# A block with a 16384-expert layer: gathered experts replaced by dense products over both tables, split fp32r products replaced by plain fp32 ones

## The reference

```python
q = (xt @ wq).reshape(t, 8, 2, 128)
scores = einsum('thpd,hpnd->thpn', q, keys)         # 8 heads, 2 halves, 128 keys
s_top, i_top = top_k(scores, 16)
cand = s_top[:, :, 0, :, None] + s_top[:, :, 1, None, :]
c_score, c_idx = top_k(cand, 16)
expert = i1 * 128 + i2                              # of 16384
gates = softmax(c_score)
a = gelu(einsum('td,thkd->thk', x, u_tab[expert]))  # 128 rows a token
y = einsum('thk,thkd->td', gates * a, v_tab[expert])
```

## Time and profile before

| | us |
|---|---|
| median of 3 runs | 1440.13 (1437.09 to 1442.69) |
| the profiled execution | 1454.04 |
| its span, first to last instruction | 1452.3 |

### The profile page before, as it was taken

The page is one execution under the profiler, slowest core; times in us unless marked ns, Lnnn a source line. Parts: engine busy times, 40 slices in busy tenths (PEclk is TensorE's granted clock), DMA queues, the critical chain, the costliest instruction groups (busy, mean ns, idle before and its releaser), DMA issues.

```text
span 1452.3 us, 13572 instructions
## 1 busy us (share of the span) xinstructions
PE 962.3 (66%) x4844; PEld 709.2 (49%) x4844; DVE 932.9 (64%) x1773; ACT 371.8 (26%) x769; POOL 634.8 (44%) x591
## 2 busy tenths in 40 slices
PE   5998996440714505566635073077899996999996
PEld 4797885110201202252511021027667784999996
DVE  3458367868887689787796985742353214888743
ACT  4544222110101101111011010012133123777632
POOL 2015027777775677778777758870001002000000
PEclk9999999785966858679868577599985588999998
DMA  4563569999999899999999989992500011555440
GB/s 161 183 181 119 211 234 391 351 356 372 342 410 336 313 372 345 344 340 337 361 364 346 398 302 319 316 376 73 193 1 0 1 55 62 174 175 174 160 160 30
DMA packets 137044, 353.60 MB, mean 243 GB/s; under 512 B 19952, under 2 KB 43664, under 8 KB 136848
## 3 DMA queue, kind: packets, MB, share of 16 engines
q0 software_dynamic: 73728, 268.47, 50.1%
q1 hardware_dynamic: 62000, 84.02, 17.1%
q10 hardware_dynamic: 1248, 0.23, 0.1%
HBM read 351.64 MB, written 1.05 MB: 243 GB/s over the span
## 4 chain that ended last, share of the span: by engine, by line
PE 41%; POOL 23%; DVE 15%; DMA 9%; issue 9%; ACT 2%; another core or an unknown queue 0%; SPq 0%; POOLq 0%; DVEq 0%; ACTq 0%
POOL high L1845 13%; POOL arena L1845 10%; PE ps L381 7%; PE ps L385 7%; PE ps L382 7%; DVE arena L1116 3%; PE ps L581 3%; DMA high<-in_v_tab,ids 2%; PE ps L595 2%; DMA high<-in_u_tab,ids 2%; PE ps L774 2%; PE ps L552 2%; PE ps L746 2%; DMA arena<-in_v_tab,ids 2%; DMA arena<-in_u_tab,ids 2%
## 5 line engine op out<-in xcount | busy, mean ns | idle before, releaser
L581 PE MATMUL ps<-high,arena 128*128 128x512 f32 x292 | 159.2, 678 | 248.5 <-ACT arena L1572 136.9
L581 PEld LDWEIGHTS ps<-high,arena 128*128 128x128 f32 x292 | 57.7, 214 | 347.2 <-ACT arena L1572 189.3
L581 PE MATMUL ps<-arena 128*128 128x512 f32 x220 | 122.8, 690 | 154.4 <-ACT arena L1572 65.7
L1093 DVE CUSTOM_DVE_ANT_0 high<-high,arena 128x1024 f32<-128x1024 f32 x145 | 177.2, 1225 | 36.2 <-DMA high<-in_u_tab,ids 31.2
L1845 POOL DMA_INDIRECT high<-in_v_tab,ids x147 | 170.5, 1160 | 60.4 <-issue 41.9
L1845 POOL DMA_INDIRECT high<-in_u_tab,ids x145 | 162.9, 1123 | 49.0 <-issue 42.5
L1845 POOL DMA_INDIRECT arena<-in_u_tab,ids x111 | 127.1, 1145 | 97.4 <-DVE arena L1041 62.7
L827 DVE TENSOR_TENSOR wl<-ring,wh 128x1024 fp32r<-128x1024 f32 (+1 forms) x100 | 120.1, 1206 | 75.3 <-ACT wh L1356 75.3
L1093 DVE CUSTOM_DVE_ANT_0 arena<-arena 128x1024 f32<-128x1024 f32 x111 | 135.7, 1226 | 34.9 <-DMA arena<-in_u_tab,ids 31.2
L581 PEld LDWEIGHTS ps<-arena 128*128 128x128 f32 x220 | 43.7, 215 | 231.1 <-issue 135.4
L1845 POOL DMA_INDIRECT arena<-in_v_tab,ids x109 | 121.8, 1117 | 47.2 <-issue 27.4
(11 more groups left out here) (309 smaller groups left out, 2068.3 us busy)
## 6 DMA issues: line engine op xcount, KB each, us to landing
ring<-in_w_ff SPq DMA_DIRECT2D x22, 1024.0 KB, 7.2
ring<-in_w_in SPq DMA_DIRECT2D x9, 2048.0 KB, 9.0
high<-in_w_in SPq DMA_DIRECT2D x4, 2048.0 KB
ring<-in_w_ff SPq DMA_DIRECT2D x4, 2048.0 KB, 8.2
ring<-in_w_out SPq DMA_DIRECT2D x2, 2048.0 KB, 8.7
ring<-in_wq SPq DMA_DIRECT2D x2, 2048.0 KB, 13.4
high<-in_wq SPq DMA_DIRECT2D x2, 2048.0 KB
ring<-in_w_o SPq DMA_DIRECT2D x2, 2048.0 KB, 9.5
```

The source lines that it names most:

```text
L581: m = e.matmul(ps[PAY[i][half]][:, :], DG[n // 2 % 2], row_buffer(u, 1, n)[:, 512 * half:512 * half + 512], start=(c == 0 and n == 1), sto ...
L1093: e.tensor_tensor_reduce(row_buffer(u, 0, n), row_buffer(u, 0, n), H2N[i], 1.0, 0.0, ALU.mult, ALU.add, AA[i][:, col:col + 1]).then_inc(*d ...
```

## The change

- The split products go. Every projection is plain fp32, with weights read from the slot where they land; L1356, L827 and the conversions of activations are gone. There are six slots for chunks of weights.
- The gathers go. Both tables are read once in order, 128 tiles of 128 experts. `dots`: a table tile is turned so that features lie on the partitions, and 8 products 128x256 give the dot products of 128 experts with 256 tokens (PSUM), of which ScalarE takes the gelu into `W`, [128 experts x tile x token]. 65 tiles (`PE_TURNS`: the first 54 and then one in seven) are turned by TensorE, eight 128x128 transposes, copied out by ScalarE; 63 by VectorE with a block transpose.
- Gates: the picks (two indices and the softmaxed score) are turned so that each token is a column. For a batch of four tokens VectorE and GpSimd make one-hot matrices of the first index (times the gate) and of the second, and TensorE multiplies them, one 128x128 product a token: entry [i2, i1] is the sum of gates of expert 128 i1 + i2. 64 batches (`GATES`) lie between pairs of tiles 13 and 51. The part for tiles whose gelu is there is multiplied in by VectorE (`pay`), the rest kept by ScalarE (`keep`) and multiplied later (`weigh`).
- Values: 128 tiles of `v_tab`, as they land, are the weights of 8 products each with `W`; all add up in four PSUM banks.
- The join and the early products are for all tokens at once, after the last value product.
- The bias loads go to ScalarE's queue, the meta tokens to SP's; h2 is brought into the order of the turned tiles by 64 small DMAs on SP.

The core of the diff (TensorE's, then VectorE's turning and payment, then SP's loads):

```diff
-                for k in range(k0, k1):
-                    e.matmul(ps[b][:, 0:N], hi[:, k - k0, :], H[:, k, :], start=(k == 0), stop=False)
-                    e.matmul(ps[b][:, 0:N], lo[:, k - k0, :], H[:, k, :], start=False, stop=False)
-                    i = e.matmul(ps[b][:, 0:N], hi[:, k - k0, :], Lo[:, k, :], start=False, stop=(k == ks - 1))
...
+                for k in range(NK):
+                    m = e.matmul(ps[n % 3][:, 0:T], slot(c)[:, k, 128 * j:128 * j + 128],
+                                 (H1T if n < 24 else MIX)[:, k, :], start=(k == 0), stop=(k == NK - 1))
...
+PE_TURNS = [n for n in range(TILES) if n < 54 or n % 7 == 5]
+GATES = [1 if 13 <= p < 26 else 2 if 26 <= p < 51 else 1 if p == 51 else 0 for p in range(TILES // 2)]
...
+            def turn_tile(n):
+                if n not in PE_TURNS:
+                    return
+                e.wait_ge(*raw_landed(n))
+                eighth = RAW[n % 4].rearrange("p (a k) -> p k a", k=8)
+                for half in HALVES:
+                    if n in turned_before:
+                        e.wait_ge(*ut_a[turned_before[n], half])
+                    for x in range(4):
+                        m = e.transpose(ps[2 + half][:, 128 * x:128 * x + 128], eighth[:, 4 * half + x, :],
+                                        ident[:, :])
+                    m.then_inc(*u_turned.on((n, half)))
+
+            def dots(n):
+                p = n // 2
+                e.wait_ge(*ut_ready(n))
...
+                for k in range(NK):
+                    m = e.matmul(ps[p % 2][:, 256 * (n % 2):256 * (n % 2) + 256], UT[n % 3][:, k, :], HP[:, k, :],
+                                 start=(k == 0), stop=(k == NK - 1))
+                m.then_inc(*a_made.on(n))
+
+            def gates(j):
...
+                for t in range(4):
+                    m = e.matmul(ps[4 + j % 2][:, 128 * t:128 * t + 128], OH2[j % 2][:, t, :], OH1[j % 2][:, t, :], start=True,
+                                 stop=True)
...
+            for n in range(TILES):
+                e.wait_ge(*v_in[n % 7][n])
...
+                for k in range(NK):
+                    o = 256 * (k % 2)
+                    m = e.matmul(ps[Y_BANK[k // 2]][:, o:o + 256], VS[n % 7][:, 128 * k:128 * k + 128], W[:, n, :],
+                                 start=(n == 0 and k % 2 == 0), stop=(n == TILES - 1 and k % 2 == 1),
+                                 skip_group_check=True)
...
+            def turn_tile(n):
+                if n in PE_TURNS or n >= TILES:
+                    return
...
+                e.transpose(UT[n % 3].rearrange("p k (b c) -> p b k c", c=32),
+                            RAW[n % 4].rearrange("p (b a k) -> p b k a", b=4, k=8)).then_inc(*ut_v.on(n))
...
+            def pay(j):
+                n = 2 * BATCHES[j] + 2
+                w = W[:, 0:n, 4 * j:4 * j + 4].rearrange("p e t -> p t e")
...
+                e.tensor_tensor(w, ps[4 + j % 2][:, :].rearrange("p (t e) -> p t e", t=4)[:, :, 0:n], w,
+                                ALU.mult).then_inc(*g_paid.on(j))
...
+            for n in range(TILES):
...
+                    e.wait_ge(*y_step[n - 7])
+                e.dma_start(VS[n % 7], v_tab[128 * n:128 * n + 128, :]).then_inc(*v_in[n % 7].on(n))
+
+            e.wait_ge(*y_step[111])
+            for c in range(6):
+                load(C_P2 + c)
+            e.wait_ge(*y_step[127])
+            e.dma_start(H0[:, :, 0:16], metaT.rearrange("(k p) t -> p k t", p=P)).then_inc(*meta_in.on("meta"))
```

More of the change, by code:

```diff
@@ L128, in build @@
[L128 to L143 removed]
+        tix = sb("tix", [P, 2 * 64], U32)
@@ new lines, in tensor @@
+            turn_tile(0)
+            for p in range(TILES // 2):
+                for n in (2 * p, 2 * p + 1):
+                    if n + 1 < TILES:
+                        turn_tile(n + 1)
+                    dots(n)
+                if p in (4, 7, 10):
+                    scores({4: 5, 7: 6, 10: 7}[p])
+                if p in (11, 28):
+                    turn_picks(p // 28)
+                for j, q in enumerate(BATCHES):
+                    if q == p:
+                        gates(j)
@@ L1122, in vector @@
-            for _ in first:
-                pass
-            for _ in join(1):
-                pass
+            gates_of(0)
+            rest_of_it = select_half(1)
+            for p in range(TILES // 2):
+                now = [j for j in range(64) if BATCHES[j] == p]
+                before = [j for j in range(64) if BATCHES[j] == p - 1]
+                turn_tile(2 * p + 2)
+                for j in now:
+                    one_hot(j)
+                for j in before:
+                    pay(j)
+                turn_tile(2 * p + 3)
+                if p:
+                    weigh(p - 1)
+                for _ in range(5 if 11 <= p < 25 else 0):
+                    next(rest_of_it, None)
+                if p == 25:
+                    gates_of(1)
@@ L1128, in linear @@
+            e.wait_ge(*rooted["pre"])
+            for k in range(8):
+                scale(("pre",), k, H0, "mix_pre", RS2, UU)
             def linear():
@@ new lines, in scalar @@
+            for p in range(TILES // 2):
+                turned_tile(2 * p + 1)
+                turned_tile(2 * p + 2)
+                gelu(p)
+                if p in (4, 7, 10):
+                    scores({4: 5, 7: 6, 10: 7}[p])
+                if p in (10, 24):
+                    exponentials(p // 24)
+                if p in (11, 28):
+                    picks(p // 28)
+                for j, q in enumerate(BATCHES):
+                    if q == p:
+                        keep(j)
+            exp_and_log()
@@ L1935, in sync @@
+            for c in range(6, 17):
+                if c - 6 < 11:
+                    e.wait_ge(*f_made[4 * (c - 6) + 3])
+                load(C_F1 + c)
             for i in HALVES:
```

1069 lines of the change are left out of this document (428 added, 641 removed).

## The result

The changed kernel takes 1777.04 us (median of 4 runs, 1768.91 to 1781.21) where the kernel before, beside it, takes 1441.41. The ratio is 1.2327 (95% interval 1.2274 to 1.238): slower by 23 per cent. The profiled execution took 1777.43 us with a span of 1775.7; the sum in the prediction was 1803 for the span, 1.5 per cent too much.

The account below looks back on a forecast made before the run. Gathers bound the expert stage, TensorE the rest; the bound moves to TensorE. 246 + 568 + 443 + 80 = 1337 against 1026 (+311), feed-forward +40: span 1803, profiled about 1805, median 1795; range 1765 to 1870 us.

Parts of the forecast that it names:

- Prices: TensorE costs read from the earlier timeline: plain 128x256 product 0.432 us, tile of eight 3.46, eight transposes 0.98.
- Part 3: First half of the experts, dots and gates: TensorE paces, other engines fit under it; 568 us together.
- Part 1: Plain products instead of split ones: first stage net +13 us, feed-forward net +40; removed conversions give nothing back by themselves.
- The middle: From 1026 to 1208 us of the kernel before, same work in same order: change of 0.
- Part 2: Queries and scores take 62.5 us, experts begin at 246; the 64 small DMAs reordering h2 cost nothing.
- Part 4: Second half of the experts, values: 128 tiles of 8 products at 0.432 us, 443 us, TensorE-bound.
- The feed-forward: 528 products grow from 0.380 to 0.458 us each, +41, less 1 for a shorter start: net +40.
- Part 5: Join standing alone after the values: gap 18 us (bounds 12 and 30), early products 59, lower clock 3; together 80.
- The second (stepped access paces): Rival: table-tile transposes and gate writes slow through stepped access; 1859 us, with both 1880; chance 0.13.
- The third (the clock falls in the turned part): Rival: first 54 expert tiles run at 1.2 GHz because of transposes, +187 us, 1982; chance 0.04.
- The fourth (the other side): Rival: experts' dense products take 0.12 instead of 0.432 us, saving 639 us and giving 1160; chance 0.01.
- The median: Profiled execution before is 1 per cent over its median; half carrying over turns about 1805 into 1795 us.

Follow-up runs that it names:

- third experiment: Changed kernel with two waits put back on ScalarE: for the first weight chunk before the first squares, for the last additions before the feed-forward's squares; 1785.62 us.
- seventh experiment: Changed kernel with all table tiles turned by TensorE and one fp32r product instead of a plain fp32 one in both halves of the experts; 1307.59 us.
- fourth: Changed kernel with the load of the meta tokens moved on SP ahead of the six weight chunks; 1764.91 us.
- sixth: Changed kernel with VectorE's turns cycling through five forms of reading and writing steps, TensorE's turns alternating stepped and contiguous reads; 1766.49 us (one run).
- eighth: Kernel with one fp32r product in both halves of the experts, plus the meta tokens' load ahead of the six weight chunks; 1275.9 us.

## Why the prediction held, and which steps did not

*The bound* (first part): right. The 740 us of the gathers became 1003 us of TensorE at clock 1.00.

*Prices.* The 256-wide plain product held: 0.43, taken from the earlier trace rows. Eight turns were priced at 0.98 from the earlier trace rows, a group of four with the change to another kind of product beside it; in a stream of eight they take 0.89. 65 tiles by 0.09 are 6 of the 7 us by which Part 3 is too high.

*Part 1*, the mis-sized term. The growth of the products was right: +20 and +41.5 with the splits kept. Of the 4 us that I let vanish in the waits between the chains 3.2 vanished: three waits of TensorE for a conversion or a low part, of 1.4, 1.0 and 0.8 us, the last of them inside the first tile's 7.5 us. What failed is "starts some 0.6 earlier and ends about 1 us earlier", and with it that the conversions "lay beside TensorE and give nothing back by themselves". The first tile starts 10.1 us earlier (22.01, now 11.86), since ScalarE's first conversion had stood ahead of the first squares and made them wait for a 2 MB chunk. The earlier trace rows showed it: TensorE's first sum waits until 13.71 for ScalarE's squares. I took that as given and didn't ask what ScalarE waited for, though its own row was in the trace: L1356, 10.1 us of idle time for the chunk. The third experiment puts that wait in again and pays 8.8 us, 1.2 of them because its chunk landed later; moving the step in the kernel before gives 5.2. And the tile, once started, ran at the full clock, where I had assumed half, as the earlier trace rows has it from 22 to 28:

```profile
11.80:17.00 5.20, 5.14 (x24) 4.55 (x25) 3.48 (x14) 0.96 (x4) 0.00 (x0) 1.00 1.05 389
```

So it took some 3.5 us and not the 7.5 of before, another 4 us. Growth 18, less 10.1, 4 and the 2.4 of the other two waits, is +1.5; measured is +1.9, against +13 in the sum. Why the clock was up here and down there, no experiment asked.

*The middle* was set at 0 and came out at -8. The squares ahead of the feed-forward stood behind the conversion of its first tile, which waited for all additions; in the changed kernel they follow the additions one by one. Putting the wait back costs 6.1 us of 46. I had given this start 1 us. The rest, 147.6 instead of 149.2 in the linear part, lies inside the spread between executions (137.5 to 149.2 for the same work). So a part of the 8 us was chance: the same kernel in an execution like the third experiment's would have shown some -18.

*Part 2* and *Part 4*: right within 1 us. The 64 small loads hid: SP had issued the last at 213.6 us, and the first table tile is turned at 235.2.

*The feed-forward*: +37.8 us (262.8 for 225.0), forecast +40. With the split steps kept it is +41.5, so some 4 us of waits went with them; two of TensorE's for low parts, 0.6 each, are in that trace and not in the changed kernel's, and the rest I didn't trace.

*Part 3*: TensorE paces, as forecast, but VectorE's sizes were guessed too small: its turn takes 2.04 us and not 1.23, its one-hot 0.353 and not 0.3, so that it is busy 33.65 of 40 us in the late part, against an estimate of 6.2 in 9.3:

```profile
680.00:720.00 40.00, 40.00 (x218) 36.08 (x217) 33.65 (x42) 6.88 (x18) 12.03 (x21) 1.00 0.43 119
```

It still hid, with a sixth of its time to spare. GpSimd's one-hot is 0.616 us, inside the bounds of 0.3 to 0.83.

*Part 5*: gap 22.1 for 18, inside 12 to 30, by the mechanism named: the meta tokens are there at 1252.51, 14.0 us after the last value product (forecast 12 to 13). The 3 us that I added to the early products for a lower clock were not there: they ran at 1.00 and took 58.7 us, 128 times 0.458. The clock was down only in the sums ahead of them.

*Rivals.* The second (stepped access paces) had its mechanism right on VectorE and its price wrong: the step costs 0.80 us a turn there, but VectorE is covered, and TensorE's turns pay nothing. The rule of 16-byte lines, which the prediction named beside it, is borne out by the runs on the one engine and made no difference in time. The third (the clock falls in the turned part) fell: 1.00 from 235 to 1238, even with all tiles turned by TensorE. By the Trainium skill (TensorE: Matmul & The Clock Gate, section "Part 4: PE-mode transpose"), where a transpose doesn't count as busy in the way that a product does, one might have feared it; in these traces eight transposes (0.89 us) beside eight products (3.45 us) left the clock at 1.00. The fourth (the other side) had the right lever and the wrong condition: the plain product is not at 0.12, but a single fp32r product is at 0.129, and then the dense form wins: 0.9135, and 0.8891 with the meta tokens first. The forecast for it was 1160 with nothing else in the way; 1307.59 came out. The difference is what took TensorE's place: 56 us for turning all tiles on TensorE, 51 in the second half (183 us of transfer against 1024 x 0.129 = 132 of products), 19 of waits for one-hots, 17 more in the gap of the join; the 4 that are left are TensorE's waits for ScalarE's copies.

*The median.* The profiled execution of after (1777.43) lies at its median (1777.04), so the surplus of 1 per cent that the profiled execution of before has did not carry over; the half of it that I took off hid 10 of the 28 us by which the sum for the profiled execution (1805) was too high. That part of the median's nearness is luck.

Left open: why the same linear part takes 147.6 us at a granted clock of 0.68 in some executions (the changed kernel, the seventh experiment) and 137.5 to 139.7 at 0.73 to 0.75 in others (the third, fourth, sixth and eighth).

## What to carry to other kernels

Before you cost the removal of a step at nothing because its engine is not the bound, look at what stands behind it on that engine and what it waits for: a conversion that waits for a large load delays every small step behind it, and here the price showed only at the serial places, the start and the norms. In this kernel dense in place of gathered work was decided by the price of one product: with the products of the experts at 0.43 us it lost 23 per cent (291 of the 323 us of span arise between the first query and the end of the early products: 1146.9 us for 855.5), with them at 0.129 it won 9, with coarser arithmetic. And when the bound moves, the order of a DMA queue is priced anew: the same small load behind the same chunks cost 10.6 us, then 27, because the lead of the queue over the work had shrunk from 24 us to 9.

## What the runs showed of the hardware

- A plain fp32 product 128x256 takes two records and 0.43 us, an fp32r product one record and 0.129. The Trainium skill (FP8 and Floating Point Precision, section "TensorE Precision Notes") has four passes for true fp32; the ratio measured is 3.3.
- VectorE's block transpose of 128x1024 takes 1.24 us when it reads at 4 or 8 bytes' step and 2.04 at 16 or 32; TensorE's transposes read every eighth element at next to no cost (eight of them in 0.90 us against 0.88 contiguous).
- VectorE rounds 128x1024 to fp32r in 0.69 us (0.815 in the mean while the value table comes in), ScalarE in 1.04; GpSimd makes a one-hot of 128x128 in 0.616 us, VectorE in 0.353.
- In the join TensorE stood idle for 11 us and the granted clock was 0.66 over the sums behind it: 5.86 us for 16 records that take 3.93 at 1.00, without the wait. After 27 us of idle time they took 6.60.
